# Rotary embedding in an attention stage: the exchange of quarters moved from a permutation matmul to transfers inside SBUF

## The reference, cut to what matters

```python
def rope_rotate(x, ang):
    m = ang.shape[-1]
    x1, x2 = x[..., :m], x[..., m:]
    c = jnp.cos(ang)[:, None, :]
    s = jnp.sin(ang)[:, None, :]
    return jnp.concatenate([x1 * c - x2 * s, x2 * c + x1 * s], axis=-1)
...
    q = rms_norm(q.reshape(b_, s_, ATTN_HEADS, HEAD_DIM), qn_g)
    k = rms_norm(k.reshape(b_, s_, KV_HEADS, HEAD_DIM), kn_g)
...
    q = apply_axial_rope(q, ang_row, ang_col)
    k = apply_axial_rope(k, ang_row, ang_col)
```

## Time and profile before

| | |
|---|---|
| median of 3 runs | 1665.84 us (1665.64 to 1667.63) |
| the profiled execution | 1665.42 us, of which the span of instructions is 1663.6 us |
| PE busy over the span | 1618.1 us, 97% |
| DVE, ACT, POOL busy | 1057.5, 668.9, 102.2 us |
| granted TensorE clock, mean | 0.993 of full speed |
| DMA | 103.85 MB, 62 GB/s in the mean |

### The profile page before, as it was taken

The page is one execution under the profiler, slowest core; times in us unless marked ns, Lnnn a source line. Parts: engine busy times, 40 slices in busy tenths (PEclk is TensorE's granted clock), DMA queues, the critical chain, the costliest instruction groups (busy, mean ns, idle before and its releaser), DMA issues.

```text
span 1663.6 us, 23794 instructions
## 1 busy us (share of the span) xinstructions
PE 1618.1 (97%) x9484; PEld 1566.3 (94%) x9484; DVE 1057.5 (64%) x1628; ACT 668.9 (40%) x1073; POOL 102.2 (6%) x59
## 2 busy tenths in 40 slices
PE   5999999999999999999999999999999999999999
PEld 5999889989999999999999888788999999999998
DVE  6432665676776577477653666668767747756764
ACT  4333224453343244144332666655424414423431
POOL 4000200000000000000122322100000000000000
PEclk7999999999999999999999999999999999999999
DMA  4122002221222222212211100022122221221222
GB/s 135 51 64 63 26 14 69 59 76 50 78 76 67 61 77 78 75 51 70 83 58 39 38 21 20 9 80 64 55 73 77 73 77 54 70 80 55 77 71 81
DMA packets 193629, 103.85 MB, mean 62 GB/s; under 512 B 3792, under 2 KB 191184, under 8 KB 193520
## 3 DMA queue, kind: packets, MB, share of 16 engines
q1 hardware_dynamic: 193040, 101.20, 21.5%
q0 software_dynamic: 144, 0.79, 0.1%
q10 hardware_dynamic: 336, 0.35, 0.1%
HBM read 99.18 MB, written 3.15 MB: 62 GB/s over the span
## 4 chain that ended last, share of the span: by engine, by line
PE 92%; DVE 4%; ACT 1%; issue 1%; DMA 0%; POOL 0%; SPq 0%; ACTq 0%; DVEq 0%; POOLq 0%
PE unit_ps L536 15%; PE unit_ps L537 14%; PE unit_ps L538 14%; PE unit_ps L819 13%; PE unit_ps L817 13%; PE unit_ps L818 13%; PE unit_ps L995 2%; PE misc_ps L682 1%; PE misc_ps L536 1%; PE misc_ps L538 1%; PE misc_ps L952 1%; PE misc_ps L537 1%; PE misc_ps L963 1%; PE unit_ps L710 1%; PE misc_ps L668 1%
## 5 line engine op out<-in xcount | busy, mean ns | idle before, releaser
L817 PE MATMUL unit_ps<-h_pair,w_hi 128*128 128x384 f32 x1232 | 412.2, 335 | 3.1 <-ACT t L1297 3.0
L819 PE MATMUL unit_ps<-h_pair,w_lo 128*128 128x384 f32 x1232 | 411.6, 334 | 0.0
L818 PE MATMUL unit_ps<-h_pair,w_hi 128*128 128x384 f32 x1232 | 411.6, 334 | 0.0
L536 PE MATMUL unit_ps<-pair_b,w_hi 128*128 128x384 f32 x960 | 323.3, 337 | 6.5 <-DVE w_lo L1429 5.0
L538 PE MATMUL unit_ps<-pair_b,w_lo 128*128 128x384 f32 x960 | 320.9, 334 | 0.0
L537 PE MATMUL unit_ps<-pair_b,w_hi 128*128 128x384 f32 x960 | 320.8, 334 | 0.0
L817 PEld LDWEIGHTS unit_ps<-h_pair,w_hi 128*128 128x128 f32 x1232 | 231.2, 188 | 4.2 <-ACT t L1297 3.6
L818 PEld LDWEIGHTS unit_ps<-h_pair,w_hi 128*128 128x128 f32 x1232 | 231.3, 188 | 0.0
L819 PEld LDWEIGHTS unit_ps<-h_pair,w_lo 128*128 128x128 f32 x1232 | 231.2, 188 | 0.0
L536 PEld LDWEIGHTS unit_ps<-pair_b,w_hi 128*128 128x128 f32 x960 | 180.2, 188 | 8.9 <-DVE w_lo L1429 6.3
L537 PEld LDWEIGHTS unit_ps<-pair_b,w_hi 128*128 128x128 f32 x960 | 180.3, 188 | 0.6
(11 more groups left out here) (241 smaller groups left out, 2109.3 us busy)
## 6 DMA issues: line engine op xcount, KB each, us to landing
w_raw<-in_w_gate SPq DMA_DIRECT2D x22, 512.0 KB, 3.9
w_raw<-in_w_up SPq DMA_DIRECT2D x22, 512.0 KB, 5.2
w_raw_more<-in_w_gate SPq DMA_DIRECT2D x22, 512.0 KB, 3.9
w_raw_more<-in_w_up SPq DMA_DIRECT2D x22, 512.0 KB, 5.2
w_raw<-in_w_down SPq DMA_DIRECT2D x24, 384.0 KB, 3.5
w_raw_more<-in_w_down SPq DMA_DIRECT2D x24, 384.0 KB, 3.6
w_raw<-in_ab_w_in SPq DMA_DIRECT2D x17, 512.0 KB, 3.9
w_raw<-in_c_w_in SPq DMA_DIRECT2D x12, 512.0 KB, 3.8
```

The source lines that it names most:

```text
L536: pe.matmul(out, w_hi, m_hi, start=start, stop=False)
L817: pe.matmul(out, hi, m_hi, start=starts and k == 0, stop=False, skip_group_check=True)
L818: pe.matmul(out, hi, m_lo, start=False, stop=False, skip_group_check=True)
L819: last = pe.matmul(out, lo, m_hi, start=False, stop=k == HK - 1, skip_group_check=True)
```

## The change

The exchange of quarters is made by transfers instead of matmuls. Per head SyncE issues four transfers, each of 32 partitions and 768 tokens (96 KB), from the head in `T[2]` or `T[3]` into `T[0]`, each quarter to the place of its neighbour (`turn_head`). They wait for the head to be read and for the sum of the head before, and stand on SyncE ahead of the load of the weights four units on (`TURN_LOADS`). The sign goes into the table of sines, and the gain columns are multiplied into the tables of cosines and sines, once for keys and once for queries, by ScalarE (`gained_ropes`); GpSimd loads the tables a second time between. VectorE then takes one product by sines over the whole head and, new on this engine, the sum, one behind the other; GpSimd keeps the product by cosines and the remainder. ScalarE's gain copy, TensorE's `rot`, and VectorE's second scaling of the query factors (now in the root's epsilon) are gone.

```diff
+TURN_LOADS = 4
...
-    _put(_at + (4 if _kind == "q" else 5), "turn", _i, 0)
-    _put(_at + (6 if _kind == "q" else 5), "turn", _i, 1)
+    if _kind == "k":
+        _put(_at + 5, "broadcast", _i)
+    _put(_at + (6 if _kind == "k" else 4), "turn", _i)
...
+            def turn_head(i):
+
+                sp.wait_ge(unit_read, reads(BASE["c"] + UNIT_OF[i]))
+                if i:
+                    sp.wait_ge(qk_sum, i)
+                for quarter in range(4):
+                    to, of = quarter * HD // 4, (quarter ^ 1) * HD // 4
+                    sp.dma_start(T[0][to:to + HD // 4, :], T[2 + i % 2][of:of + HD // 4, :]).then_inc(turn_landed, 16)
...
                     for n, (kind, _, c) in enumerate(C_UNITS):
+                        if n - TURN_LOADS in UNIT_OF:
+                            turn_head(UNIT_OF.index(n - TURN_LOADS))
...
-            def turn(i, half):
-
-                pe.wait_ge(qk_gain, i + 1)
-                pe.wait_ge(root_done, CHAIN["qk"] + i + 1)
-                if QK[i][1] == "q" and half:
-                    pe.wait_ge(rot_read, 2 * i + 1)
-                bank = 0 if QK[i][1] == "k" and half else 3
-                pe.matmul(misc_ps[:, bank, 0:HALF], rot, T[2 + i % 2][:, half * HALF:(half + 1) * HALF],
-                          start=True, stop=True).then_inc(rot_done, 1)
...
-                    act.wait_ge(qk_sum, i)
-                act.activation(T[1][:, :], T[0][:, :], ACT.Square).then_inc(qk_sq, 1)
...
-                act.activation(T[2 + i % 2][:, :], T[0][:, :], ACT.Copy, scale=cols[:, col:col + 1]).then_inc(qk_gain, 1)
+                    act.wait_ge(colsum_done, CHAIN["qk"] + i)
+                act.activation(T[1][:, :], T[2 + i % 2][:, :], ACT.Square).then_inc(qk_sq, 1)
...
+            def gained_ropes(kind, turn):
+
+                act.wait_ge(rope_landed, 16 * turn)
+                for part, col in enumerate((COL[kind + "n"], COL[kind + "n_turned"])):
+                    act.activation(ropes[:, part, :], ropes[:, part, :], ACT.Copy,
+                                   scale=cols[:, col:col + 1]).then_inc(rope_gained, 1)
...
+                if slot == 8 * (UNIT_OF[KVH] + 1) - 4:
+                    gained_ropes("q", 2)
...
-                dve.tensor_scalar(q_scale[:, QK[i][2], :], q_scale[:, QK[i][2], :], HD ** -0.5, None,
-                                  ALU.mult).then_inc(q_scaled, 1)
...
-                dve.tensor_tensor(T[1][:, tokens], misc_ps[:, bank, 0:HALF], ropes[:, 1, tokens], ALU.mult).then_inc(rot_read, 1)
...
+                dve.wait_ge(turn_landed, 4 * 16 * (i + 1))
+                dve.wait_ge(rope_gained, 2 if QK[i][1] == "k" else 4)
+                dve.tensor_tensor(T[0][:, :], T[0][:, :], ropes[:, 1, :], ALU.mult).then_inc(turn_scaled, 1)
+                dve.wait_ge(turn_scaled, i + 1)
+                dve.wait_ge(qk_cos, i + 1)
+                dve.tensor_tensor(T[4][:, :], T[4][:, :], T[0][:, :], ALU.add).then_inc(qk_sum, 1)
...
+                if i == KVH:
+
+                    pool.wait_ge(qk_sum, KVH)
+                    load_ropes()
...
-                pool.tensor_tensor(T[4][:, :], T[4][:, :], T[1][:, :], ALU.add).then_inc(qk_sum, 1)
```

More of the change, by code:

```diff
@@ L272, in trunk_kernel @@
         rstd = at("rstd", [2, HALF], rstd_at)
[L273 removed]
+        tab = at("tab", [3, P], fresh(3 * P * 4))
         cols = at("cols", [N_COL], fresh(N_COL * 4))
@@ L999, in between @@
             def between(slot):
-                for what, i, *half in PLAN.get(slot, ()):
+                for what, i in PLAN.get(slot, ()):
                     if what == "sums":
                         head_sums(i)
[L1003 to L1006, removed]
+                    elif what == "broadcast":
+                        broadcast(CHAIN["qk"] + i)
                     elif what == "scores":
@@ L1390, in result_hi @@
                 act.activation(pairB[:, h, 0, s0:s0 + ln], values_bank[:, 0:ln], ACT.Copy).then_inc(pv_hi, 1)
+            def gained_ropes(kind, turn):
[3 more added lines that the diff above has]
+                                   scale=cols[:, col:col + 1]).then_inc(rope_gained, 1)
             root_of(CHAIN["c"], D)
+            gained_ropes("k", 1)
             for slot in range(SLOTS):
                 j = slot // 8 - 1
-                for what, i, *half in PLAN.get(slot, ()):
+                if slot == 8 * (UNIT_OF[KVH] + 1) - 4:
+                    gained_ropes("q", 2)
+                for what, i in PLAN.get(slot, ()):
                     if what == "flip":
@@ L1872, in evacuate_half @@
                 else:
-                    if not half and UNIT_OF.index(j):
-                        dve.wait_ge(qk_gain, UNIT_OF.index(j))
-                    done = dve.tensor_tensor(T[0][:, half * HALF:(half + 1) * HALF], ps, rstd[:, half, :], ALU.mult)
+                    i = UNIT_OF.index(j)
+                    if i >= 2:
+                        dve.wait_ge(qk_sq, i - 1)
+                        dve.wait_ge(qk_cos, i - 1)
+                        dve.wait_ge(turn_landed, 4 * 16 * (i - 1))
+                    done = dve.tensor_tensor(T[2 + i % 2][:, half * HALF:(half + 1) * HALF], ps, rstd[:, half, :], ALU.mult)
                 done.then_inc(unit_read if half else half_read, 1)
@@ L1937, in _ @@
                     elif what == "turn":
-                        turned(i, *half)
+                        turned(i)
                     elif what == "scores":
@@ L2008, in _tables @@
     backward = same & (i[:, None] >= i[None, :])
-    rot = np.zeros((P, P))
-    q = HD // 4
-    for half in (0, HD // 2):
-        for k in range(q):
-            rot[half + q + k, half + k] = -1.0
-            rot[half + k, half + q + k] = 1.0
-    return np.concatenate([ident, forward, backward, rot], axis=1).astype(np.float32)
+    return np.concatenate([ident, forward, backward], axis=1).astype(np.float32)
 def _rope():
@@ L2026, in _rope @@
             pos = (t // GRID_W if d < half else t % GRID_W).astype(np.float32)
-            rows.append(fn(pos * inv[d % (half // 2)]))
+            sign = -1 if fn is np.sin and d % half < half // 2 else 1
+            rows.append(sign * fn(pos * inv[d % (half // 2)]))
         out.append(np.stack(rows))
@@ L2058, in tiles, with exchanged @@
         return np.asarray(v).reshape(-1, P).T
-    eps = np.full((P, 1), EPS, np.float32)
+    eps = np.tile(np.array([EPS, HD * EPS], np.float32), (P, 1))
+    def exchanged(v):
+        return np.asarray(v).reshape(2, 2, HD // 4)[:, ::-1].reshape(P, 1)
     columns = np.concatenate([tiles(ab_norm[0]), tiles(ffn_norm[0]), tiles(c_norm[0]), tiles(ffn_norm[1]),
                               tiles(gla_out_norm[0]), tiles(c_q_norm[0]), tiles(c_k_norm[0]), tiles(gla_bias_f[0]),
-                              tiles(gla_bias_b[0]), eps], axis=1)
+                              tiles(gla_bias_b[0]), eps, exchanged(c_q_norm[0]), exchanged(c_k_norm[0])], axis=1)
     up_pad = np.zeros((2 * RANK, 4 * P), np.float32)
```

52 lines of the change are left out of this document (24 added, 28 removed).

## The result

The changed kernel takes 1656.84 us (median of 7 runs, 1656.06 to 1661.95) where the kernel before takes 1665.84 (7 runs, 1665.53 to 1668.88). The ratio of the runs is 0.9943, with a 95% interval of 0.9929 to 0.9957: 9.5 us less, between 7.2 and 11.8. 1657.1 us were forecast. A second comparison, further down, gave 0.9938. Ratios are formed from fast runs alone; one execution of 6917.09 us, of the kernel with the weights in slot 2, is left out of its ratio.

The account below looks back on a forecast made before the run. TensorE was taken to bound the attention stage, with VectorE's crowded slots next. Gains of 3.9 + 0.5 + 0 + 2.4 + 1.0 + 0.9 = 8.7 us gave 1657.1 us against the 1665.84 median; range 1651.0 to 1661.6.

Parts of the forecast that it names:

- k1: Second key head: no scores beside it, so no transpose waits and its two turns leave TensorE, 1.30 us gained.
- score wait behind q0: Before the first query head's first scores: TensorE's 0.5 us wait for GpSimd's remainder goes, as the sum ends earlier.
- q1: Second query head: only 0.58 us of slack before the probabilities' transpose, so TensorE waits 1.32 us and nothing is gained.
- q7: Last query head, beside shorter output units: no slack, but old waits on slowed scalings and ScalarE's copy shrink, net 0.9 us.
- What leaves TensorE: Turns as matmuls on TensorE: 0.65 us each, 10.4 us for query heads, 2.6 for keys, 13.0 us in all.
- What VectorE gets: Slot 4 of a query head: product and sum back to back take 1.98 us, so the weights' split starts 0.60 us later.
- The wait of 0.70 us: Steady query head: TensorE waits 0.70 us for scaled probabilities before transposing them, so it gains 0.60 us, not 1.30.
- Transfers: Four SyncE transfers per head, one per about 0.5 us: the last lands about 4.3 us after the read, costing nothing.
- The port's rate: Transfers over partitions 0 to 31 reach 8 of 16 ports, half rate; the four would land about 0.8 us later.
- VectorE has room: Rival: TensorE never waits for VectorE's product and sum; 14.7 us gained, 1651.1 us. Chance 0.20.
- VectorE paces the heads: Rival: VectorE's chain takes 0.6 us more per head; later query heads give nothing, 4.4 us remain, 1661.4 us. Chance 0.14.
- Collision on the port: Rival: GpSimd's product still runs when VectorE's pair starts, 1.85 us more on seven heads, 4.3 us slower, 1670.1. Chance 0.03.

Follow-up runs that it names:

- second comparison: The unmodified changed kernel rerun on one chip with its version splitting weights in slot 2, both against the kernel before: 1659.34 us, ratio 0.9938; the other 1651.91 us, 0.9906.
- the kernel with the weights in slot 2: Changed kernel with ScalarE's and VectorE's split of the next unit's weights moved from slot 4 to slot 2 of a query unit: 1653.02 us; again 1651.91 us.
- first group: Edits to the changed kernel: product and sum in slot 2, 1659.12 us; half as wide, 1653.74; sum on GpSimd, 1666.78; weights split in slot 2, 1653.02.
- the kernel with 24 transfers: Changed kernel with every transfer cut into six along the tokens, 24 of 16 KB per head in place of 4 of 96 KB: 1724.87 us (one run).
- 16 transfers: Changed kernel with every transfer cut into four along the tokens, 16 of 24 KB per head in place of 4 of 96 KB: 1669.22 us (one run).

## Why the prediction was right, step by step

TensorE's column sums mark a head's progress. The lead of the changed kernel over the one before grew between them by the amounts in the third column (behind q7's, up to the last read of the output units).

| part | predicted | measured |
|---|---|---|
| k0 | 1.30 | 1.30 |
| k1 | 1.30 | 1.54 |
| q0 | 1.30 | 1.29 |
| score wait behind q0 | 0.5 | 0.77 |
| q1 | 0 | -0.02 |
| q2 and q3 | 1.20 | 1.20 |
| q4, q5 | 0.60, 0.60 | 0.58, 0.62 |
| q6 | 1.0 | 1.05 |
| q7 | 0.9 | 1.04 |
| sum | 8.7 | 9.4 |

For the score wait, TensorE's matmul ahead of q0's first scores and the second matmul of those scores, before and, below it, now:

```profile
921.01 0.34 PE L538 MATMUL unit_ps<-pair_a,w_lo 128*128 128x384 f32 x1
...
922.18 0.39 PE L537 MATMUL misc_ps<-kpair,pair_b 128*128 128x512 f32 x1
```

```profile
920.31 0.33 PE L554 MATMUL unit_ps<-pair_a,w_lo 128*128 128x384 f32 x1
...
920.71 0.40 PE L553 MATMUL misc_ps<-kpair,pair_b 128*128 128x512 f32 x1
```

- **What leaves TensorE**: 0.65 us per turn stood. A steady head took 21.00 us and takes 19.74 when VectorE is out of the way: 1.26 for two turns, 1.30 predicted.
- **What VectorE gets**: the durations were right (0.95 and 0.96 us, the second 0.99 behind the first, as in the earlier trace rows), the room they take was a little less. I moved the split by 1.98 us for the pair; it starts 0.87 us behind the sum's start, not 0.99, as it doesn't need the result. So slot 4 grew by 0.48 us, not 0.60.
- **The wait of 0.70 us** is 20.41 - 19.74 = 0.67. The listed waits give only 0.43, since the list counts idle time from the end of the matmul before (989.57 + 0.34 = 989.91). In the run with the weights in slot 2 the transpose starts 0.18 us behind the start of that matmul; here it is 990.34 - 989.57 = 0.77, so 0.59 are lost there, and the matmuls behind it start 0.06 later than usual. What left TensorE was 0.04 too large in the forecast and the wait 0.03, so their difference came out at 0.59 for 0.60. That is in part luck: with the measured sizes the sum of the prediction, 0.48 + 1.26 - 1.25 and 0.06 for the handover, gives a wait of 0.55 us, and it holds no term for the slower matmuls behind a wait. Each run of the first group confirms the cause: slot 4 0.94 longer, heads 0.94 longer; 0.47 shorter, 0.47 to 0.49 shorter; below that TensorE's 19.74.
- **The score wait and q1**: from the matmul ahead of q0's first scores to their second matmul it took 1.17 us and takes 0.40 (the rows above). So the wait that is listed with 0.5 us cost 0.77, more than its listing for the same reasons as above. From there to q2's column sums it takes 13.90 us before and 13.92 now: at q1 nothing is gained, as forecast. Its listed wait is 1.05 us, and 929.17 - 927.79 = 1.38 between starts, less the usual 0.18 and with 0.06 behind it, makes 1.26 lost, what the two turns gave.
- **k1**: 0.24 us more than worked out. From the matmul ahead of its broadcast to the L537 behind the turns it took 3.20 us before (881.65 to 884.85), where k0 took 2.99 (869.31 to 872.30); now both take 1.69. Before, the broadcast started 0.05 us behind the end of a reciprocal that followed a split of 2.03 us on VectorE: a short wait that the prediction didn't count. No run was made on why it is gone.
- **q7**: 1.04 us for 0.9, also in part luck. Most of ScalarE's 0.9 us was to go, but 0.76 are left, and a wait of 0.45 us for VectorE's remainder of a result (L1938) is new. Against that the wait at step 1 grew only from 0.17 to 1.27 us, where 1.30 + 0.60 were counted, and the waits of 0.67 and 0.32 us behind it went.
- **Transfers**: landing 4.0 us behind the read, 5.0 at q1; 4.3 were forecast. The issues took 0.6 us each, not the 0.5 of the earlier trace rows. At q0 there were 5.4 us to land in.
- **The port's rate**: 96 KB over 32 partitions land in 2.1 us, beside 2.2 for the 128 KB of the earlier trace rows; 24 KB land in 1.8. The rule of the Trainium skill (page SBUF — State Buffer, section Door 1: The DMA port swizzle), by which such a transfer reaches half of the ports, is neither shown nor refuted by landings that differ by 0.3 us. The 0.8 us that it was estimated to cost four transfers did not show: they landed 0.3 us ahead of the forecast, which had counted the last issue's own time apart from its landing.
- **The rivals**: "VectorE has room" describes the stage once the weights are split in slot 2, not the change as it stands. "VectorE paces the heads" fell: a steady head did get shorter. "Collision on the port" did not happen to the query heads, since GpSimd's product ends slots ahead of the pair; at k1 it did, where the product took 1.71 us beside GpSimd's, at no cost seen. What it would cost is shown by the sum on GpSimd: the split waited out most of it. The Trainium skill, page SBUF — State Buffer, section Who interferes with whom, says of VectorE instructions with two inputs in SBUF that they contend with a GpSimd instruction that reads SBUF; the 2.64 and 2.20 us rows agree.

## What to carry to other kernels

Work taken off the pacing engine is worth its full duration only where the engine next in line has slack at the same instruction: before summing the gain, find the wait that comes next and subtract. An engine that idles a third of a stage can still be full in the slots that matter; moving one unrelated operation (here a split of weights) out of those slots brought 5.5 us more, where the change had brought 9.4; 2.4 of them it would have brought without the change. Where an operation on another engine holds VectorE up, as GpSimd's sum held the split here, giving it away can cost more than keeping it.

## What was not expected of the hardware

A VectorE instruction that meets GpSimd is recorded as a longer one, not as idle time: 1.22 us became 2.64, 0.95 became 2.20, each ending 0.8 to 1.1 us behind the end of GpSimd's. In a list of busy times this looks like work.

In the kernel with 24 transfers, TensorE's granted clock is 1.00 from 1006 to 1011 us, ahead of the wait of 3.11 us before the transpose of step 1, and 0.76 on average in the 5 us from 1016 us on, between its two levels of 1.2 and 2.4 GHz, though TensorE is then busy throughout; it is 1.00 in the 5 us behind that. The steady heads still grew by the lateness of the transfers alone. Where TensorE paces the stage such stretches show in the time: by estimate 4 us with 16 transfers and 1.7 with the sum on GpSimd.

The small transfers inside SBUF were here priced by their issue: 96, 24 and 16 KB land within 2.1, 1.8 and 1.8 us, but SyncE issued one per 0.6 to 0.67 us.
